# A mixer's entry: the second tokens' moments by a sum in the adding step and ScalarE's squares, and the latents' low parts cut and placed otherwise

## What is computed

```python
# first block, the end of its last layer
x = layer_norm(ALPHA * x + sq_relu_mlp(x, mlp_w1[i], mlp_b1[i], mlp_w2[i], mlp_b2[i]),
               ln_g[i, 2], ln_b[i, 2])
# layer_norm: mu = mean(x), var = mean((x - mu)**2), (x - mu) * rsqrt(var + 1e-5) * g + b
# second block, its entry
mod = c_act @ w_ada[l] + b_ada[l]
h = rms_norm(x, g_mix[l]) * (1.0 + sc_a) + sh_a     # x * rsqrt(mean(x*x) + 1e-6) * g
proj = h @ w_in                                      # 1024 x 2240
dq, dk, dv, q_lat, kv_lat, k_rope = jnp.split(proj, IN_SPLITS, axis=-1)
```

## Time and profile before

| | |
|---|---|
| three executions | 963.14, 963.54, 963.59 us; median 963.54 |
| the profiled execution | 963.24 us, its span 961.4 us |
| PE busy | 947.7 us, 99% of the span |
| PE's weight loads | 811.7 us, 84% |
| DVE busy | 685.5 us, 71% |
| ACT busy | 518.4 us, 54% |
| POOL busy | 54.0 us, 6% |
| granted TensorE clock | 0.998 of full speed |
| moved by DMA | 202.48 MB, 211 GB/s on average |

### The profile page before, as it was taken

How to read it: one execution, slowest core, us unless ns; L and a number is a source line. 1 busy time by engine, 2 the same in 40 slices (tenths; PEclk the granted TensorE clock), 3 DMA queues, 4 the chain that set the end, 5 groups by cost and what they waited for, 6 DMA issues and landing times.

```text
span 961.4 us, 12979 instructions
## 1 busy us (share of the span) xinstructions
PE 947.7 (99%) x5062; PEld 811.7 (84%) x5062; DVE 685.5 (71%) x932; ACT 518.4 (54%) x732; POOL 54.0 (6%) x95
## 2 busy tenths in 40 slices
PE   9999999999999999999999999998999999999996
PEld 8889888888888888888788888887988888888885
DVE  6955568658878775885788877668677886556555
ACT  6656563535655555354275555547566575444543
POOL 0000121001000002100000000002100000000000
PEclk9999999999999999999999999999999999999999
DMA  9965275626988885284289888773631566655521
GB/s 324 346 219 176 88 271 188 220 88 234 343 278 283 289 294 198 74 296 140 90 307 322 290 291 295 241 233 130 230 122 55 176 216 200 215 179 188 177 74 45
DMA packets 109884, 202.48 MB, mean 211 GB/s; under 512 B 4172, under 2 KB 76124, under 8 KB 106496
## 3 DMA queue, kind: packets, MB, share of 16 engines
q1 hardware_dynamic: 106656, 189.67, 58.5%
q0 software_dynamic: 3024, 11.72, 3.4%
q10 hardware_dynamic: 144, 0.26, 0.1%
HBM read 200.58 MB, written 1.06 MB: 210 GB/s over the span
## 4 chain that ended last, share of the span: by engine, by line
PE 90%; DVE 6%; ACT 2%; issue 1%; POOL 0%; DMA 0%; POOLq 0%; DVEq 0%; SPq 0%; ACTq 0%
PE WB L359 20%; PE YB L384 11%; PE YB L377 10%; PE YB L392 10%; PE WB L362 10%; PE YB L438 4%; PE WB L377 2%; PE WB L384 2%; PE WB L392 2%; PE WB L341 2%; PE WB L344 2%; PE WB L348 2%; PE WB L698 1%; PE WB L717 1%; DVE U L1946 1%
## 5 line engine op out<-in xcount | busy, mean ns | idle before, releaser
L1713 DVE TENSOR_TENSOR wl<-raw,wh 128x2048 fp32r<-128x2048 f32 (+1 forms) x146 | 334.1, 2296 | 119.1 <-ACT wh L1105 116.9
L1105 ACT CAST wh<-raw 128x2048 fp32r<-128x2048 f32 (+1 forms) x150 | 285.2, 1905 | 31.4 <-PE YB L392 8.9
L359 PE MATMUL WB<-XS,wh 128*128 128x512 f32 x832 | 208.1, 392 | 0.0
L359 PEld LDWEIGHTS WB<-XS,wh 128*128 128x128 f32 x832 | 152.3, 189 | 29.0
L362 PEld LDWEIGHTS WB<-XS,wl 128*128 128x128 f32 x832 | 113.5, 190 | 8.1
L362 PE MATMUL WB<-XS,wl 128*128 128x256 f32 x832 | 116.0, 283 | 0.0
L377 PE MATMUL YB<-wh,FHT 128*128 128x512 f32 x352 | 109.1, 391 | 0.0
L384 PE MATMUL YB<-wl,FHT 128*128 128x512 f32 x352 | 108.7, 390 | 0.0
L392 PE MATMUL YB<-wh,FLT 128*128 128x512 f32 x352 | 108.6, 390 | 0.0
L1279 ACT COPY U<-WB 128x256 f32<-128x256 f32 x102 | 33.1, 376 | 132.7 <-PE WB L362 132.7
L384 PEld LDWEIGHTS YB<-wl,FHT 128*128 128x128 f32 x352 | 66.1, 188 | 14.1
(11 more groups left out here) (339 smaller groups left out, 1208.1 us busy)
## 6 DMA issues: line engine op xcount, KB each, us to landing
raw<-in_mlp_w SPq DMA_DIRECT2D x64, 1024.0 KB, 5.3
raw<-in_w_ada_t SPq DMA_DIRECT2D x24, 1024.0 KB, 5.0
raw<-in_mlstm_w_in SPq DMA_DIRECT2D x11, 1024.0 KB, 7.6
raw<-in_w_ffn_down SPq DMA_DIRECT2D x11, 1024.0 KB, 5.0
raw<-in_w_ffn_gate SPq DMA_DIRECT2D x10, 1024.0 KB, 5.4
raw<-in_w_ffn_up SPq DMA_DIRECT2D x10, 1024.0 KB, 5.7
raw<-in_mem_w_kv SPq DMA_DIRECT2D x8, 1024.0 KB, 5.2
raw<-in_xattn_wq SPq DMA_DIRECT2D x8, 1024.0 KB, 7.5
```

The lines of the kernel that those rows point to most:

```text
L359: e.matmul(W[:, :], H[:, at(k)], XS[:, k, :], start=k == 0, stop=False)
L1105: f = e.copy(w[:, 0:a * b], raw[:, 0:a * b])
L1713: f = e.tensor_tensor(L[:, 0:a * b], raw[:, 0:a * b], H[:, 0:a * b].bitcast(F32), ALU.subtract)
```

## The change

For the second tokens (t = 1) of `n12` the moments are made in another way. `sums` replaces `head`: the adding instruction also writes the sum of its row (`accum_out`), and two one-column operations make of the two halves' sums minus the mean, and minus the mean over 32. ScalarE's `variance` squares (u - mean) / 32 over each half and sums it, and GpSimd's `var_stats` adds both and the epsilon and takes the inverse root. `centre` gets the mean as an argument and waits for the square of its half. The squares stand first in `mix_between`, ahead of the high part of `lat 2`.

On DVE the low part of `lat 0` is no longer made whole at the end of `mlp`: its first half stands ahead of the first tokens' `head`, its second behind `sums(1, 0)`. The low part of `lat 1` moves from ahead of `evac(0, 1)` to behind the third low pair of t = 0; the fourth low pair, both centrings and then both scalings follow. The low part of `lat 2` is cut into three quarters and one quarter instead of two halves.

```diff
--- before.py
+++ after.py
@@ -1410,7 +1410,16 @@
                 e.wait_ge(*dve_ln["x", "12", t, h])
                 rms_half("mix", t, h)
 
+            def variance(h):
+
+                w, cs = cols(("ln", "12", 1), 8), slice(512 * h, 512 * h + 512)
+                e.wait_ge(*dve_ln["mean", "12", 1])
+                e.activation(JX["mix"][1][:, cs], U[:, 1, cs], ACT.Square, bias=w[:, 3:4], scale=1 / 32,
+                             accum_out=w[:, 4 + h:5 + h]).then_inc(act_ln.add(("var", "12", 1, h)))
+
             def mix_between():
+                variance(0)
+                variance(1)
                 hi_to(M["lat", 2])
                 mix_square(1, 0)
                 mix_square(1, 1)
@@ -1713,11 +1722,12 @@
                         f = e.tensor_tensor(L[:, 0:a * b], raw[:, 0:a * b], H[:, 0:a * b].bitcast(F32), ALU.subtract)
                     f.then_inc(w_lo.add(m_))
 
-            def lo_half(m, h):
+            def lo_half(m, h, parts=(1, 1)):
 
                 n = mms[m]
-                size = chunks[n][2] * chunks[n][3] // 2
-                cs = slice(size * h, size * h + size)
+                size = chunks[n][2] * chunks[n][3]
+                first = size * parts[0] // sum(parts)
+                cs = slice(first, size) if h else slice(0, first)
                 e.wait_ge(*w_hi[m])
                 f = e.tensor_tensor(WL[m % NS][:, cs], RAW[n % NR][:, cs], WH[m % NS][:, cs].bitcast(F32), ALU.subtract)
                 if h == 1:
@@ -1940,11 +1950,30 @@
                         e.tensor_scalar(BN[:, t, 13:14], BN[:, t, 13:14], LN_EPS, None, ALU.add
                                         ).then_inc(dve_ln.add(("var", s, t)))
 
-                def centre(self, t, h):
+                def sums(self, t, h):
+
+                    s, cs, w = self.s, slice(512 * h, 512 * h + 512), cols(("ln", self.s, t), 8)
+                    e.wait_ge(*self.x_in(t, h))
+                    e.wait_ge(*pe_rows[self.rows, t, h])
+                    p = e.scalar_tensor_tensor(U[:, t, cs], X[:, t, cs], ALPHA, YB[2 * t + h][:, :], ALU.mult, ALU.add,
+                                               accum_out=w[:, h:h + 1])
+                    p.then_inc(dve_ln.add(("u", s, t, h)))
+                    if h == 1:
+                        e.wait_ge(*dve_ln["u", s, t, 1])
+                        e.tensor_scalar(w[:, 2:3], w[:, 0:1], w[:, 1:2], -1 / 1024, ALU.add, ALU.mult)
+                        e.tensor_scalar(w[:, 3:4], w[:, 0:1], w[:, 1:2], -1 / 32768, ALU.add, ALU.mult
+                                        ).then_inc(dve_ln.add(("mean", s, t)))
+
+                def centre(self, t, h, mean=None):
+
                     s, cs = self.s, slice(512 * h, 512 * h + 512)
                     e.wait_ge(*self.g_in)
-                    e.scalar_tensor_tensor(U[:, t, cs], U[:, t, cs], BN[:, t, 12:13], BV[self.g][:, cs],
-                                           ALU.subtract, ALU.mult).then_inc(dve_ln.add(("c", s, t, h)))
+                    if mean is not None:
+                        e.wait_ge(*dve_ln["mean", s, t])
+                        e.wait_ge(*act_ln["var", s, t, h])
+                    e.scalar_tensor_tensor(U[:, t, cs], U[:, t, cs], BN[:, t, 12:13] if mean is None else mean,
+                                           BV[self.g][:, cs], ALU.subtract if mean is None else ALU.add, ALU.mult
+                                           ).then_inc(dve_ln.add(("c", s, t, h)))
 
                 def scale(self, t, h):
                     s, cs = self.s, slice(512 * h, 512 * h + 512)
@@ -2079,7 +2108,8 @@
                                                ).then_inc(dve_mlp.add(("b2", i, t, h)))
                     if late and j == 14:
                         late()
-                lo_to(M["w2", i, 14 if tail == 2 else 13] + 3)
+                if tail == 2:
+                    lo_to(M["w2", i, 14] + 3)
 
             layer_norm(0, 0, "wout", lambda t, h: (d_x[t], 16))
             lo_to(M["wout", 3] + 3)
@@ -2128,27 +2158,30 @@
                                 ).then_inc(dve_ln.add(("z", s, t, h)))
 
             g, b = lambda k: MC[:, 8 + k:9 + k], lambda k: MC[:, k:k + 1]
+            lo_half(M["lat", 0], 0)
             n12.head(0, 0)
             n12.head(0, 1)
             n12.first()
-            n12.head(1, 0)
+            n12.sums(1, 0)
+            lo_half(M["lat", 0], 1)
             rms_z("mix", 0, 0)
             rms_z("mix", 0, 1)
-            lo_to(M["lat", 1])
             evac("mix", 0, 1, g, b)
-            n12.head(1, 1)
+            n12.sums(1, 1)
             rms_low("mix", 0, 0)
             rms_low("mix", 0, 1)
             rms_low("mix", 0, 2)
-            n12.centre(1, 0)
+            lo_to(M["lat", 1])
+            mean = cols(("ln", "12", 1), 8)[:, 2:3]
+            rms_low("mix", 0, 3)
+            n12.centre(1, 0, mean)
+            n12.centre(1, 1, mean)
             n12.scale(1, 0)
-            rms_low("mix", 0, 3)
-            n12.centre(1, 1)
             n12.scale(1, 1)
-            lo_half(M["lat", 2], 0)
+            lo_half(M["lat", 2], 0, (3, 1))
             rms_z("mix", 1, 0)
             rms_z("mix", 1, 1)
-            lo_half(M["lat", 2], 1)
+            lo_half(M["lat", 2], 1, (3, 1))
             evac("mix", 1, 1, g, b)
             evac("mix", 1, 3, g, b)
             for q in range(4):
@@ -2498,6 +2531,13 @@
 
 
 
+            def var_stats(s, t):
+
+                w = cols(("ln", s, t), 8)
+                e.wait_ge(*act_ln["var", s, t, 1])
+                step(e.tensor_scalar(w[:, 6:7], w[:, 5:6], w[:, 4:5], LN_EPS, ALU.add, ALU.add))
+                rsqrt(BN[:, t, 14:15], w[:, 6:7], po_ln.add(("r", s, t)))
+
             def ln_stats(s, ts=(0, 1)):
                 for t in ts:
                     e.wait_ge(*dve_ln["var", s, t])
@@ -2557,9 +2597,10 @@
             e.dma_start(g_rows.rearrange("a (p k) -> p a k", k=8), gates).then_inc(d_gate, 16)
             e.wait_ge(d_gate, 16)
             e.dma_start(GB[:, :, :], g_rows.partition_broadcast(128)).then_inc(d_gate, 16)
-            for t in range(2):
-                ln_stats("12", (t,))
-                rms_stats("mix", (t,))
+            ln_stats("12", (0,))
+            rms_stats("mix", (0,))
+            var_stats("12", 1)
+            rms_stats("mix", (1,))
```

## The result

The changed kernel took 964.95 us (median of 22 executions, 963.95 to 966.69) against 963.57 for the kernel before (22, 963.14 to 964.34): ratio 1.0013, interval 1.0007 to 1.0019. It is 1.4 us slower in the median and lies above the predicted range, 962.2 to 964.5 around 963.7.

What follows compares the result with a forecast made beforehand. TensorE, working 99% of the span, bounds the kernel; only its holes before `kl 1`'s low weights count. Those come 0.13 us later: 963.24 profiled + 0.13 + 0.30 to the median = 963.67, so 963.7, range 962.2 to 964.5.

Steps and rivals of the forecast that it cites:

- Part 1: First low part halved, one half behind the first tokens' norm: second adding at 645.09 instead of 645.70, 0.61 us gained.
- part 2: First tokens' statistic: GpSimd held by the low half's reading until 651.14, z(0) at 652.12 instead of 651.41; 0.61 us gain gone.
- The two waits of VectorE behind z(0): Evacuation waits for PE's second pair, +0.53 us; second sum waits for the last product before the turn's second half, +0.41.
- The sum with accumulator: Second tokens' adding that writes its row sum runs at full rate: 0.61 us, accumulator read 0.08; at half rate 964.8.
- The last quarter: Low part of `lat 2` behind z(1): 0.5 us less than the half, so `ql`'s five products no longer wait 0.37.
- part 4: GpSimd held again by three quarters of `lat 2`: z(1) at 664.16, 0.25 later; `kl 1`'s low weights 667.92, 0.13 us later.
- cover 0.15 us, thin: Second tokens' root on GpSimd, asked at 658.7, done at 660.2, before the first scaling at 660.35.
- part 3: VectorE from z(0) to the last scaling: 8.89 us instead of 9.23, last scaling at 661.01, only 0.24 earlier.
- The slower rival: Second tokens' root gets through only behind the second centring, ends at 660.9, all 0.5 us later: 964.2; chance 0.15.
- The wait of VectorE before the first scaling: Sign of being wrong: a hole of DVE before the second tokens' first scaling would show the late root.
- z(1) to the low weights: From z(1) to `kl 1`'s low weights on PE: 3.76 us instead of 3.88, bound by ScalarE's copy of the third pair.
- merge into one of 1.5 to 2 us: Sign of being right: PE's holes become one of that length before the turn of the second tokens.

Runs made afterwards that it cites:

- swap: Changed kernel with the second half of the first low part (`lat 0`) ahead of `sums(1, 0)` instead of behind it: 964.71 us.
- root_free: Changed kernel with the second tokens scaled by the first tokens' inverse root, without waiting for their own; all operations still run: 964.11 us.
- after_again: The changed kernel itself, timed once more beside the other experiments: 964.09 us.
- long_hole: Changed kernel with the first 1440 columns of `lat 2`'s low part made twice, lengthening TensorE's hole to 3.59 us: 968.40 us.
- fill: Changed kernel with eight unneeded 512-column products in TensorE's hole ahead of the turn of the second tokens: 964.77 us.
- even: Changed kernel with the low part of `lat 2` in two halves again instead of three quarters and one quarter: 964.61 us.
- cuts_only: Changed kernel with the moments' edits undone; low parts' pieces and places as changed: 965.18 us, ratio 1.0015 to the kernel before.
- moments_only: Changed kernel with the low parts' edits undone; second tokens' moments as changed: 962.98 us, ratio 0.9994 to the kernel before.
- three: Changed kernel with the edits of swap and even, and the sum of the two squares moved from GpSimd to VectorE: 963.13 us.
- four: Changed kernel with `lat 0`'s second half ahead of `sums(1, 0)`, `lat 1`'s low part back ahead of the evacuation, `lat 2` in halves: 962.37 us.
- four_again: The kernel of four, timed once more: 962.97 us, ratio 0.9994 to the kernel before.
- four_filled: The kernel of four with five unneeded 512-column products ahead of the turn of the second tokens: 963.10 us.
- long_hole_filled: The kernel of long_hole with fourteen unneeded 512-column products inside the hole: 966.13 us.

## Why the prediction was wrong

*Right.* The table sets its steps beside the changed trace, as distances from the landmark (643.45, now 643.83).

| step | before | forecast | measured |
|---|---|---|---|
| second adding | 2.25 | 1.64 | 1.64 |
| z(0) | 8.57 | 8.67 | 8.66 |
| last scaling | 17.80 | 17.56 | 18.20 |
| z(1) | 20.46 | 20.71 | 21.36 |
| low weights of kl 1 | 24.34 | 24.47 | 25.22 |

(The last scaling is the second of the pair at 661.36, 0.67 behind its start.) Part 1 and part 2 hold to 0.01 us, and swap shows the cause: the neighbour's reading holds GpSimd. The two waits of VectorE behind z(0), which I had as 0.53 and 0.41 from starts of PE, are 0.35 and 0.40 by the idle time of their rows, but the second adding starts 2.69 behind z(0), as forecast (2.70). The sum with accumulator costs about 0.61, its read 0.08 to 0.09, as the row said. The Vector Engine (DVE) Microarchitecture Reference in the Trainium skill (section "Points that are easy to get wrong") says that this form with two such sources in SBUF runs at half the rate. Line 1700, 1.22 us for 1024 columns, doesn't bear it out; the sum has one source in PSUM and doesn't test it. The last quarter is hidden, and z(1) to the scaling before it keeps the 3.15 us of part 4 (665.19 - 662.03 = 3.16).

*The step that failed: "cover 0.15 us, thin".* In part 3 I let the root of the second tokens end at 660.2 with a margin, though I had just shown that one operation can be held for as long as its neighbour reads. Here GpSimd asks while VectorE has three two-input instructions in a row: the trace has the low pair and both centrings without a gap of 0.1 us. In the time of the kernel before (0.38 less) GpSimd was asked at 658.86 instead of 658.7, took 2.04 instead of 1.5, and was done at 660.90 instead of 660.2, 0.55 past the cover. The slower rival named exactly this, with a root that ends at 660.9, and priced it at 0.5 us (964.2); the trace shows 0.64 at the last scaling, root_free 0.60 in the seam. I gave it 0.15. The wait of VectorE before the first scaling, which I had named as a sign of being wrong, is the 0.51 of the row at 661.36. The rule used in parts 2 and 4 for two statistics had to be used for the third as well; then it is the likeliest case, and the sum is 963.67 + 0.6 = 964.3. The trace of the kernel before even had a root held by a centring, which I overlooked; POOL, then DVE, before:

```profile
647.62 0.99 POOL L2481 TENSOR_TENSOR BN<-BN,SM 128x1 f32<-128x1 f32 x1 [8.60 <-DVE BN L1940]
```
```profile
647.45 1.41 DVE L1946 SCALAR_TENSOR_TENSOR U<-U,BN,bv 128x512 f32<-128x512 f32 x2
```

The first tokens' root took 0.99 instead of 0.56 beside their centrings. A mechanism that is certain at two places isn't a rival at the third.

*A small term mis-sized:* z(1) to the low weights, forecast 3.76, measured 3.86. ScalarE's copy of the third pair in the changed kernel:

```profile
668.20 0.41 ACT L1256 CAST XS<-S 128x256 fp32r<-128x256 f32 x1
```

It ends at 668.61, 3.42 behind z(1), where I had 3.41. But the start and the two products behind it take 0.44 (668.61 to 669.05), not 0.35.

*What the sum left out: the clock.* I wrote that the holes "merge into one of 1.5 to 2 us" and counted only its length. It is 2.29 us, and behind such a hole TensorE is granted less in part of the executions: 0.65 in swap's window, 0.84 and 0.73 in after_again's, 0.50 in long_hole's behind 3.59 us. The stretch in after_again cost 1.16 us. The forecast had not asked what a longer pause would do. Over the 33 executions of the changed kernel in both runs the mean is 964.79, that of the 20 at 0.998 is 964.40, and that of the 26 at 0.997 or 0.998 is 964.53: 0.3 to 0.4 us for the clock on average. It is less sure than the seam's loss, since fill, without any low clock, was at 964.69.

Together: 963.67 + 0.64 + 0.10 = 964.4 for the seam, and 0.3 to 0.4 for the clock, against medians of 964.95 and 964.09. The seam's 0.88 us are shown, and their causes, by swap, root_free and even. How much of the rest is the clock and how much the scatter of the start is open; one run's median gives no fixed number.

## What to carry to other kernels

In these traces a one-column operation of GpSimd that was asked for while VectorE read from two SBUF tensors was held until that reading ended: place long subtractions where no statistic is asked for, or cut and order them so that a one-input or a PSUM instruction stands there (swap: 0.98 to 0.38 us by exchanging two instructions). Where it is asked for within a row of such instructions, take it as held, and give the cover its price at that bound. Ask, too, what a longer pause of TensorE does to its clock: the kernel before, with holes under 0.8 us, had none of 107 executions at 0.996 or less, and the changed kernel and swap, with one hole of 2.3 us, had 15 of 44.

And measure from a landmark just ahead of the change: the start of these executions scattered by 1.3 us, more than anything that the change did, while the distances behind the landmark repeat to some hundredths.

## What the runs showed of the hardware that was not expected

A GpSimd operation pending behind two-input VectorE instructions didn't get in at each boundary: with starts 0.34 us apart (659.10, 659.44) it passed one, and it got in behind the first centring, an instruction of 512 columns, though the second stood ready. SBUF — State Buffer in the Trainium skill (section "SBUF: two separate sides") has the lock itself, an instruction of VectorE with two SBUF inputs and one of GpSimd that reads SBUF shutting each other out for a whole instruction, and the traces agree for GpSimd's side (0.98, 1.03, 1.56 us); which of several boundaries in a row lets it in is open. In cuts_only it was the root that was held (1.56 us), the operation before it having begun 0.38 us ahead of the low half.

Executions with a mean clock of 0.996 or less, by the hole ahead of the second turn: 1 of 44 with 1.3 us (moments_only, three, four, four_again), 1 of 33 with 1.7 to 1.8 (even, root_free, cuts_only), 15 of 44 with 2.3 (the changed kernel twice, swap), 5 of 5 with 3.6, and none of 107 before. With the hole filled by products that nobody needs it was none of 11 in fill and in four_filled and 1 of 10 in long_hole_filled. At 0.997 there are 6 of 44, 6 of 33, 6 of 44 and none of 5, and 10 of 107 before; some hold a low stretch (after_again's) and some don't (cuts_only's). So the share grows with the hole, but no length parts it cleanly, and the same kernel gave 7 of 22 and 0 of 11. The price isn't one number either: 1.16 us in after_again's trace, about 1.0 in swap's, 1.85 in long_hole's, and 2 and more by the times in four and four_again. I have no row that explains that.
